# One encoder layer on one core: w_glu and p_ssm by seven block products, GpSimd's weight sums ahead of its gates

## The chip, the cores and the metric

The kernel runs on one core of a Trainium2 chip. The time is the device time of that core for one execution, in microseconds; the median of three runs is given. The engines are TensorE (PE, with PEld for its weight loads), VectorE (DVE), ScalarE (ACT), GpSimd (POOL) and SyncE (SP, which issues the loads).

## What is computed

One layer of a hybrid encoder over 512 prompt tokens and 64 sample tokens, 1024 channels. The part that the change touches:

```python
y_ssm = jax.nn.gelu(y_ssm + lp['ssm_d'].astype(jnp.float32) * u32)
y_ssm = (y_ssm * jax.nn.sigmoid(y_ssm @ lp['w_glu'])).astype(x.dtype)
mixed = jax.nn.sigmoid(g_s) * (y_ssm @ lp['p_ssm']) + jax.nn.sigmoid(g_a) * (att @ lp['p_att'])
x = x + rmsnorm(mixed @ lp['w_out'], lp['norm_mix_post'])
...
x = x + rmsnorm(jnp.square(jax.nn.relu(h @ lp['w_ff1'])) @ lp['w_ff2'], lp['norm_ff_post'])
```

w_glu and p_ssm are 1024 x 1024. Everything is float32.

## The kernel before

Products are made in fp32r: each operand is split into a high part (H, cut by ScalarE) and a low remainder (L, by VectorE), and a product is three matmuls, H x H, H x L and L x H. A weight is worked through in slabs of 128 output channels (128 x 1024 numbers, 512 KB). SyncE loads a raw slab into a slot `wraw`; ScalarE cuts it (`split_h`, L963), VectorE makes the remainder (`split_l`, L1663), and TensorE waits for `wl_done`. Four slabs of halves `wH`, `wL` rotate. Tokens are split into two halves of 288 (`HT`). `gemm` (L2401) makes one slab: 8 blocks of the depth x 3 x 2 halves = 48 matmuls.

The stages around the change, one after the other on TensorE: p_att, then w_glu (`T_GLU`, 8 slabs), then p_ssm (`T_PSSM`, 8 slabs), then w_out. In w_glu, ScalarE takes the sigmoid of slab j (L1310), VectorE multiplies it with y, which lies in `z` (L1982), and both cut the result y2 into `aH`, `aL` (L1013, L1677), the input of p_ssm. `z` is stored by time within a chunk, so its reads step through it (`by_time`). In p_ssm, VectorE multiplies the slab with the sigmoid of a gate that SyncE brings back from memory (L1989), adds the attention branch `m1` (L1992), and both cut the mixed result into `uH`, `uL`, the input of w_out. During the first w_out slab ScalarE squares the memory rows `memr` (L1323), which TensorE then transposes. GpSimd has no work in these stages.

In three of the four quarters of the feed-forward part a pair of w_ff1 slabs is made by seven block products instead of eight (`pair_products`, L3140): the pair is a 2 x 2 block matrix (two slabs x two halves of the depth), the tokens are two halves, and sums of blocks are multiplied. A product is 12 matmuls. GpSimd forms four sums of raw weight blocks into `comb` (T3, T2, T1, T4, L911 to L919), and ScalarE and VectorE cut six operands a pair: RA (a whole slab), T2, T1, T3, RB1 and T4 (half slabs). VectorE joins the products into the outputs, ScalarE copies one of them (p_1) out of PSUM (L1591).

Every engine works through its own list in order; waits on semaphores tie them.

## Time and profile before

| | |
|---|---|
| time, median of 3 runs | 1140.31 us (1140.18 to 1142.34) |
| span of the profiled execution | 1137.1 us |
| PE busy | 1122.3 us |
| DVE busy | 728.0 us |
| ACT busy | 574.5 us |
| POOL busy | 253.2 us |

The profiled execution's own time is not listed apart from its span. The span runs from the first to the last instruction; the time has about 3 us more. An engine's busy time is a sum over the whole program, in which stages with different limits follow each other. A row of a timeline has the start, the length and the instruction with its tiles (out<-in); "[x <-y]" is the idle time before it and what ended it. Instructions of one engine overlap a little, so their starts can be closer than their lengths.

### The profile page before, as it was taken

Reading aid. Unit: us, or ns where it says so; the run is one execution under the profiler, and the core shown is the slowest. Engines: PE = TensorE matmul, PEld = TensorE weight load, DVE = VectorE, ACT = ScalarE, POOL = GpSimd, SP = SyncE. Lnnn points to the kernel's source line nnn. Section 1 sums busy time; section 2 is a strip of 40 time slices with the busy share of each in tenths; the row PEclk is TensorE's granted clock in tenths of the full one; section 3 lists DMA queues with packets and bytes.
Section 4 is the critical chain, followed back from the end, with each engine's and each line's share of the span. In section 5 each row is a group of like instructions: output and inputs, shape, how many; then the busy total and the mean of one; then the engine's idle time right before and its main releaser. Section 6 shows DMA issues by size and latency. Waiting matters only on the chain.

```text
span 1137.1 us, 20194 instructions
## 1 busy us (share of the span) xinstructions
PE 1122.3 (99%) x8160; PEld 1039.2 (91%) x8160; DVE 728.0 (64%) x1195; ACT 574.5 (51%) x1084; POOL 253.2 (22%) x211
## 2 busy tenths in 40 slices
PE   9999999999999999999999999999999999999997
PEld 8999999999779999998889988899889889989986
DVE  6465899997784645554774463574859438626845
ACT  6564666654797533344655342554237416614642
POOL 1066888871110000000000000000044025013203
PEclk9999999999999999999999999999999999999999
DMA  9453336455103543353556204214422323242152
GB/s 218 136 145 86 98 97 174 137 152 169 44 2 99 174 132 94 116 180 107 177 157 208 70 19 130 74 40 167 117 68 76 112 74 95 74 129 68 56 174 84
DMA packets 154141, 128.76 MB, mean 113 GB/s; under 512 B 15712, under 2 KB 127264, under 8 KB 153728
## 3 DMA queue, kind: packets, MB, share of 16 engines
q1 hardware_dynamic: 142560, 114.76, 34.4%
q10 hardware_dynamic: 11488, 12.70, 3.3%
q8 instruction: 65, 1.06, 0.4%
q14 instruction: 28, 0.23, 0.1%
HBM read 110.73 MB, written 16.84 MB: 112 GB/s over the span
## 4 chain that ended last, share of the span: by engine, by line
PE 82%; ACT 7%; DVE 4%; POOL 2%; issue 2%; ACTq 2%; DMA 1%; POOLq 0%; DVEq 0%
PE gp L2416 24%; PE gp L2822 13%; PE sp L2822 13%; PE gp L3140 6%; PE sp L3140 6%; PE gp L2899 4%; PE gp L2726 3%; PE gp L3093 2%; PE sp L3058 1%; ACT sc L1237 1%; PE sp L2726 1%; ACTq L1114 1%; PE sp L2929 1%; ACT raw L1050 1%; POOL raw L809 1%
## 5 line engine op out<-in xcount | busy, mean ns | idle before, releaser
L1663 DVE TENSOR_TENSOR wL<-wraw,wH 128x1024 fp32r<-128x1024 f32 x139 | 180.9, 1303 | 156.8 <-ACT wH L963 154.4
L963 ACT ACTIVATE wH<-wraw 128x1024 fp32r<-128x1024 f32 x139 | 146.4, 1054 | 202.6 <-PE sp L2822 46.0
L2416 PE MATMUL gp<-aH,wH 128*128 128x288 f32 (+2 forms) x800 | 173.5, 298 | 0.0
L2416 PE MATMUL gp<-aH,wL 128*128 128x288 f32 (+2 forms) x800 | 171.4, 296 | 0.0
L2416 PE MATMUL gp<-aL,wH 128*128 128x288 f32 (+2 forms) x800 | 171.2, 296 | 0.0
L911 POOL TENSOR_TENSOR comb<-wraw 128x512 f32<-128x512 f32 x12 | 16.3, 1355 | 645.2 <-DMA wraw<-in_w_ff 578.3
L2416 PEld LDWEIGHTS gp<-aH,wH 128*128 128x128 f32 x800 | 129.3, 189 | 1.9 <-issue 1.8
L2416 PEld LDWEIGHTS gp<-aL,wH 128*128 128x128 f32 x800 | 129.8, 189 | 0.0
L2416 PEld LDWEIGHTS gp<-aH,wL 128*128 128x128 f32 x800 | 129.8, 189 | 0.0
L2822 PE MATMUL gp<-wH,fH 128*128 128x512 f32 x208 | 81.2, 390 | 0.0
L2822 PE MATMUL gp<-wL,fH 128*128 128x512 f32 x208 | 80.9, 389 | 0.0
L2822 PE MATMUL sp<-wH,fH 128*128 128x512 f32 x192 | 74.7, 389 | 0.0
L2822 PE MATMUL sp<-wL,fH 128*128 128x512 f32 x192 | 74.7, 389 | 0.0
L2822 PE MATMUL sp<-wH,fL 128*128 128x512 f32 x184 | 71.6, 389 | 0.0
L2260 DVE TENSOR_TENSOR wL<-comb,wH 128x512 fp32r<-128x512 f32 x48 | 38.4, 822 | 44.5 <-ACT wH L1565 44.5
L1565 ACT ACTIVATE wH<-comb 128x512 fp32r<-128x512 f32 x48 | 29.0, 622 | 56.6 <-PE sp L2822 47.4
L2822 PE MATMUL gp<-wH,fL 128*128 128x512 f32 x136 | 52.9, 389 | 0.0
L2822 PEld LDWEIGHTS gp<-wL,fH 128*128 128x128 f32 x208 | 39.1, 188 | 7.8
L2822 PEld LDWEIGHTS gp<-wH,fH 128*128 128x128 f32 x208 | 39.1, 188 | 7.8
L820 POOL TENSOR_TENSOR prod<-fb,btab 128x256 f32<-128x256 f32 x32 | 40.3, 1279 | 17.4 <-PE sp L2522 10.3
L2822 PEld LDWEIGHTS sp<-wL,fH 128*128 128x128 f32 x192 | 36.0, 188 | 7.5
L2822 PEld LDWEIGHTS sp<-wH,fH 128*128 128x128 f32 x192 | 36.0, 188 | 7.5
(549 smaller groups left out, 2839.7 us busy)
## 6 DMA issues: line engine op xcount, KB each, us to landing
wraw<-in_w_ff SPq DMA_DIRECT2D x64, 512.0 KB, 4.3
wraw<-in_w_in SPq DMA_DIRECT2D x36, 512.0 KB, 4.2
gates_scratch<-sq ACTq DMA_DIRECT2D x16, 288.0 KB, 2.2
gate<-gates_scratch SPq DMA_DIRECT2D x16, 288.0 KB, 4.2
wraw<-in_p_att SPq DMA_DIRECT2D x8, 512.0 KB, 4.2
wraw<-in_w_glu SPq DMA_DIRECT2D x8, 512.0 KB, 4.0
wraw<-in_p_ssm SPq DMA_DIRECT2D x8, 512.0 KB, 3.8
wraw<-in_w_out SPq DMA_DIRECT2D x8, 512.0 KB, 3.9
```

What stands on the lines that cost most here:

```text
L820: last = g.tensor_tensor(prod[:, i, :, 0:SB, :], fa, ba, ALU.mult)
L911: g.tensor_tensor(block("T3"), rb[:, 4:8, :], rb[:, 0:4, :], ALU.subtract).then_inc(comb_ready, 1)
L963: s_.activation(halves_of(t, j)[0][:], wraw[w][:], ACT.Copy).then_inc(wh_done, 1)
L1565: s_.activation(wH[i][:, k0:k1, :], operand_source(p, name), ACT.Copy).then_inc(wh_done, 1)
L1663: v.tensor_tensor(low[:], wraw[w][:], high[:], ALU.subtract).then_inc(wl_done, 1)
L2260: v.tensor_tensor(wL[i][:, k0:k1, :], operand_source(p, name), wH[i][:, k0:k1, :], ALU.subtract).then_inc(wl_done, 1)
L2416: last = mm(gp[:, b + h, 0:n], w[:, k, :], y[:, k, c0:c0 + n], start=(k == 0 and w is wH[s] and y is xh), stop=(k == KT - 1 and w is wL[s]))
L2726: last = mm(dst, w[:, k, :], y[:, k, :], start=(k == 0 and w is wH[j % 4] and y is xh), stop=(k == KT - 1 and y is xl))
L2822: last = mm(dst, y, wk, start=(k == 0 and m == 0), stop=(k == KT - 1 and m == len(passes) - 1))
L2899: last = mm(KV_BANK[n][m], y[:, k, c], w[:].rearrange("p k c -> p (k c)")[:, 512 * kk:512 * kk + 512], start=(k == 0 and w is wH[i] and y ...
L3093: last = mm(d[:, h, 0:HT], w[:, k, :], y[:, k, h * HT:(h + 1) * HT], start=(k == 0 and w is wH[s] and y is bH), stop=(k == KT - 1 and w is ...
L3140: last = mm(bank[name], w[:, k0 + k, :], y[:, kk + k, c], start=(name not in ("RA1", "RB1", "T4") and k == 0 and w is wH[i] and y is yH), ...
```

## The change

Of the four pairs of slabs of w_glu and of p_ssm, the first is still made slab by slab (`gemm`), and the other three by seven block products each, as in the feed-forward part. The pairs are numbered in one row: n = 0 to 2 in w_glu, 3 to 5 in p_ssm, 6 to 17 in the feed-forward part; in the loops below p = n + 1 and p = n - 2.

The products now add up in PSUM: RA0, then T2, T3 and T4 go into one bank on top of each other, T1 and RB1 into another. Between them ScalarE copies what has been reached (`keep`: p1 after RA0, p16 after T2, p5 after T1), and TensorE waits for p1 before T2, for p16 before T3, for p5 before RB1, and for VectorE's join "22" before T4. VectorE has three joins (11, 22, 12), ScalarE writes the fourth block itself (`out_21`). The feed-forward pairs use this order as well.

Sums of token blocks (S1 to S4) are formed from `z`: S1 and S3 by GpSimd, S2 and S4 by VectorE, and cut by ScalarE and VectorE. T1 is now summed in place in the raw slab. GpSimd also takes over the multiplication with the gate, in w_glu into `z` itself (`gate_ssm`), in p_ssm in `gate_out`. In each turn of its loop two weight sums (T3, T2) stand ahead of the two gates and two (T1, T4) behind. The cuts of y2 read `z`. Two more raw slots (`wraw5`, `wraw6`) take every other pair of slabs; a slot is loaded again when its pair's RB1 is cut and T4 summed (`wait_raw`). The gates of p_ssm are sigmoided in place. The memory rows are loaded near the end of p_ssm. Some semaphores are merged, and `in_order` makes the cut of an odd or even slab from 2 on wait for both gates of its pair.

```diff
-            for j in range(8):
-                free = (evac_dve, 8 + j - 1) if j < 2 else (evac_act, ACT_BEFORE[T_GLU] + j - 1)
-                gemm(T_GLU + j, j, bH, bL, free, IN_Y if j == 0 else None)
-            for j in range(8):
-                free = (evac_act, ACT_BEFORE[T_PSSM] + j - 1) if j < 2 else (evac_dve, 8 + j - 1)
-                gemm(T_PSSM + j, j, aH, aL, free, IN_Y2 if j == 0 else None)
+        def in_order(j):
+            return j + (2 if j >= 2 and j % 2 == 0 else 1)
...
+            def pair_products(n):
+                s, p, bank = stage(n), number(n), pair_bank(n)
+                xH, xL = ((bH, bL), (aH, aL), (bH, bL))[s]
+                lower, upper = slice(0, HT), slice(HT, TT)
+                turned = (xH, xL, 0, upper)
+                if s < 2:
+                    sums = {"T2": (zsH["S2"], zsL["S2"], 0, lower), "T1": (zsH["S1"], zsL["S1"], 0, lower),
+                            "T3": turned, "RB1": (zsH["S4"], zsL["S4"], 0, lower)}
+                else:
+                    sums = {"T2": (sumH[0], sumL[0], 0, lower), "T1": turned, "T3": (sumH[1], sumL[1], 0, lower),
+                            "RB1": (sumH[2], sumL[2], 0, lower)}
+                left = {"RA0": (xH, xL, 0, lower), "RA1": (xH, xL, 4, lower), "T4": (xH, xL, 4, upper), **sums}
+                dst = dict(zip(PRODUCTS, (bank[i] for i in (0, 1, 0, 2, 0, 2, 0))))
+                for name in PRODUCTS:
+                    operand = {"RA0": "RA", "RA1": "RA"}.get(name, name)
+                    pe.wait_ge(wl_done, operand_at(n, operand))
+                    if s < 2 and p == 1 and name in ("T2", "T1", "T3", "RB1"):
+                        pe.wait_ge(suml_done, 4 * s + {"T2": 1, "T1": 2, "RB1": 3, "T3": 4}[name])
+                    if name == "T2":
+                        pe.wait_ge(*kept_at(n, "p1"))
+                    if name == "T3":
+                        pe.wait_ge(*kept_at(n, "p16"))
+                    if name == "RB1":
+                        pe.wait_ge(*kept_at(n, "p5"))
+                    if name == "T4":
+                        pe.wait_ge(*join_at(n, "22"))
+                    i, k0, _ = operand_place(n, operand)
+                    k0 += 4 * (name == "RA1")
+                    yH, yL, kk, c = left[name]
+                    for k in range(4):
+                        for w, y in ((wH[i], yH), (wH[i], yL), (wL[i], yH)):
+                            last = mm(dst[name], w[:, k0 + k, :], y[:, kk + k, c],
+                                      start=(name in ("RA0", "RA1", "T1") and k == 0 and w is wH[i] and y is yH),
+                                      stop=(k == 3 and w is wL[i]), skip_group_check=True)
+                    last.then_inc(gemm_done, 1)
+            for j in range(2):
+                gemm(T_GLU + j, j, bH, bL, ((evac_dve, 8 + j - 1),), IN_Y if j == 0 else None)
+            pe.wait_ge(evac_dve, 8)
+            pair_products(0)
+            pe.wait_ge(evac_act, ACT_BEFORE[T_GLU] + 2)
+            pair_products(1)
+            pair_free(0)
+            pair_products(2)
+            for j in range(2):
+                gemm(T_PSSM + j, j, aH, aL, (join_at(1, "12"), (out21_done, 2)), IN_Y2 if j == 0 else None)
+            pair_free(2)
+            pair_products(3)
+            pe.wait_ge(evac_dve, DVE_BEFORE[T_WOUT])
+            pair_products(4)
+            pair_free(3)
+            pair_products(5)
...
@@ ScalarE, w_glu and p_ssm @@
-            for j in range(8):
-                split_h(T_GLU + j + AHEAD, j + AHEAD)
-                act.wait_ge(gemm_done, T_GLU + j + 1)
-                s_.activation(halves(raw[:, j % 2]), result(j), ACT.Sigmoid).then_inc(evac_act, 1)
-                cut_h(aH[:, j, :], sq[:, j % 2])
...
+            def keep(n, name):
+                product, dst, bank, use = {"p1": ("RA0", p_1, 0, "11"), "p16": ("T2", p_16, 0, "12"), "p5": ("T1", p_5, 2, "22")}[name]
+                act.wait_ge(gemm_done, product_at(n, product))
+                if n:
+                    act.wait_ge(*join_at(n - 1, use))
+                s_.activation(dst[:], pair_bank(n)[bank], ACT.Copy).then_inc(kept, 1)
+            def out_21(n, kind):
+                act.wait_ge(gemm_done, product_at(n, "T4"))
+                if n < 3:
+                    act.wait_ge(gated, 2 * number(n))
+                elif n < 6:
+                    act.wait_ge(mixed_ready, 2 * number(n))
+                s_.activation(raw[:, 0, HT:TT], pair_bank(n)[0], kind).then_inc(out21_done, 1)
+            def pair_sigmoid(n, e):
+                if e:
+                    act.wait_ge(*join_at(n, "22"))
+                    act.wait_ge(*join_at(n, "12"))
+                    s_.activation(raw[:, 1], raw[:, 1], ACT.Sigmoid).then_inc(evac_act, 1)
+                else:
+                    act.wait_ge(*join_at(n, "11"))
+            def y2_h(j):
+                act.wait_ge(gated, in_order(j))
+                s_.activation(aH[:, j, :].rearrange("p (c s) -> p c s", s=SB), by_time(z[:, j, :]), ACT.Copy).then_inc(in_h, 1)
+            z_sum_h(0, "S1")
+            z_sum_h(0, "S2")
+            z_sum_h(0, "S4")
+            glu_sigmoid(0)
+            operand_h(0, "T2")
+            y2_h(0)
+            operand_h(0, "T1")
+            operand_h(0, "T3")
+            glu_sigmoid(1)
+            z_sum_h(0, "S3")
+            operand_h(0, "RB1")
+            operand_h(0, "T4")
+            y2_h(1)
+            for p in (1, 2, 3):
+                n = p - 1
+                keep(n, "p1")
+                if p > 1:
+                    y2_h(2 * p - 1)
+                if p < 3:
+                    operand_h(n + 1, "RA")
+                else:
+                    split_h(T_PSSM, 0)
+                keep(n, "p16")
+                if p > 1:
+                    y2_h(2 * p - 2)
+                if p < 3:
+                    operand_h(n + 1, "T2")
+                else:
+                    split_h(T_PSSM + 1, 1)
+                pair_sigmoid(n, 0)
+                keep(n, "p5")
+                if p < 3:
+                    operand_h(n + 1, "T1")
+                    operand_h(n + 1, "T3")
+                else:
+                    gate_sig(8)
+                    gate_sig(9)
+                pair_sigmoid(n, 1)
+                if p < 3:
+                    operand_h(n + 1, "RB1")
+                    operand_h(n + 1, "T4")
+                else:
+                    operand_h(n + 1, "RA")
+                    operand_h(n + 1, "T2")
+                out_21(n, ACT.Sigmoid)
+            y2_h(7)
+            y2_h(6)
...
@@ GpSimd @@
+            def combine(n, names=("T3", "T2", "T1", "T4")):
+                ra, rb = pair_raw(n)
+                def free(name):
+                    if n not in (0, 6):
+                        pool.wait_ge(wl_done, operand_at(n - 1, name))
+                def block(name):
+                    return operand_source(n, name)
+                if "T3" in names:
+                    for t in (TWINS[n], TWINS[n] + 1):
+                        pool.wait_ge(w_loaded[raw_slot(t)], 16 * raw_uses(t))
+                    free("T3")
+                    g.tensor_tensor(block("T3"), rb[:, 4:8, :], rb[:, 0:4, :], ALU.subtract).then_inc(comb_ready, 1)
+                if "T2" in names:
+                    free("T2")
+                    pool.wait_ge(comb_ready, comb_at(n, "T3"))
+                    g.tensor_tensor(block("T2"), block("T3"), ra[:, 0:4, :], ALU.add).then_inc(comb_ready, 1)
+                if "T1" in names:
+                    g.tensor_tensor(block("T1"), rb[:, 0:4, :], ra[:, 0:4, :], ALU.subtract).then_inc(comb_ready, 1)
+                if "T4" in names:
+                    free("T4")
+                    pool.wait_ge(comb_ready, comb_at(n, "T2"))
+                    g.tensor_tensor(block("T4"), ra[:, 4:8, :], block("T2"), ALU.subtract).then_inc(comb_ready, 1)
+            def z_sum_1(i):
+                g.tensor_tensor(timed(zsum["S1"]), z_block(0, 1), z_block(1, 1), ALU.add).then_inc(z13_ready, 1)
+            def z_sum_3(i):
+                g.tensor_tensor(timed((bS3, uS3)[i]), z_block(0, 0), z_block(0, 1), ALU.subtract).then_inc(z13_ready, 1)
+            def gate_ssm(j):
+                p, e = j // 2, j % 2
+                if p == 0:
+                    pool.wait_ge(evac_act, ACT_BEFORE[T_GLU] + j + 1)
+                    pool.wait_ge(sum_ready, 2)
+                else:
+                    pool.wait_ge(*((evac_act, ACT_BEFORE[T_GLU] + 2 + p) if e else (out21_done, p)))
+                y = by_time(z[:, j, :])
+                g.tensor_tensor(y, raw[:, e].rearrange("p (c s) -> p c s", s=SB), y, ALU.mult).then_inc(gated, 1)
+            def gate_out(p, e):
+                n = 2 + p
+                if e:
+                    pool.wait_ge(*join_at(n, "12"))
+                else:
+                    pool.wait_ge(*join_at(n, "11"))
+                    pool.wait_ge(out21_done, n + 1)
+                pool.wait_ge(gsig_ready, 8 + 2 * p + e + 1)
+                g.tensor_tensor(raw[:, e], raw[:, e], gate[:, e], ALU.mult).then_inc(gated, 1)
+            pool.wait_ge(in_h, IN_Y + 1)
+            pool.wait_ge(gemm_done, g_count(T_PATT + 1))
+            z_sum_1(0)
+            pool.wait_ge(gemm_done, g_count(T_GLU))
+            z_sum_3(0)
+            combine(0, ("T3", "T2"))
+            gate_ssm(0)
+            combine(0, ("T1", "T4"))
+            gate_ssm(1)
+            for p in (1, 2, 3):
+                combine(p, ("T3", "T2"))
+                if p > 1:
+                    gate_ssm(2 * p - 1)
+                    gate_ssm(2 * p - 2)
+                combine(p, ("T1", "T4"))
+            gate_ssm(7)
+            gate_ssm(6)
+            pool.wait_ge(gemm_done, g_count(T_PSSM))
+            pool.wait_ge(gated, 8)
+            z_sum_1(1)
+            z_sum_3(1)
+            for p in (1, 2, 3):
+                if p < 3:
+                    combine(3 + p, ("T3", "T2"))
+                if p > 1:
+                    gate_out(p - 1, 1)
+                    gate_out(p - 1, 0)
+                if p < 3:
+                    combine(3 + p, ("T1", "T4"))
+            gate_out(3, 1)
+            gate_out(3, 0)
@@ VectorE @@
+            z_sums_24(0)
+            z_sum_l(0, "S2")
+            z_sum_l(0, "S1")
+            operand_l(0, "T2")
+            y2_l(0)
+            z_sum_l(0, "S4")
+            operand_l(0, "T1")
+            operand_l(0, "T3")
+            z_sum_l(0, "S3")
+            operand_l(0, "RB1")
+            operand_l(0, "T4")
+            y2_l(1)
+            for p in (1, 2, 3):
+                n = p - 1
+                if p > 1:
+                    y2_l(2 * p - 1)
+                if p < 3:
+                    operand_l(n + 1, "RA")
+                else:
+                    split_l(T_PSSM, 0)
+                if p > 1:
+                    y2_l(2 * p - 2)
+                out_11(n)
+                if p < 3:
+                    operand_l(n + 1, "T2")
+                    operand_l(n + 1, "T1")
+                else:
+                    split_l(T_PSSM + 1, 1)
+                out_22(n)
+                if p < 3:
+                    operand_l(n + 1, "T3")
+                out_12(n)
+                if p < 3:
+                    operand_l(n + 1, "RB1")
+                    operand_l(n + 1, "T4")
+                else:
+                    operand_l(n + 1, "RA")
+                    operand_l(n + 1, "T2")
+            y2_l(7)
+            y2_l(6)
...
@@ SyncE @@
+            def wait_raw(t):
+                before = raw_before(t)
+                n = pair_of(before)
+                if n is None:
+                    sp.wait_ge(wl_done, w_count(before + 1))
+                else:
+                    sp.wait_ge(wl_done, operand_at(n, "RB1"))
+                    sp.wait_ge(comb_ready, comb_at(n, "T4"))
+            def load_w(t, s, src):
+                assert s == raw_slot(t)
+                if t == T_GLU + 3:
+                    sp.wait_ge(evac_dve, 8)
+                elif t >= 2 and t != T_GLU + 2:
+                    wait_raw(t)
+                sp.dma_start(wraw[s][:], src).then_inc(w_loaded[s], 16)
```

In the lists below `p` is one of the copies p_1, p_16, p_5, `aH<-z` a cut of y2, `wH<-zcomb` a cut of a weight sum. ScalarE before, w_glu from the third slab on:

```order
L1310 ACTIVATE raw<-gp 128x576
L1013 ACTIVATE aH<-sq 128x576
L1292 ACTIVATE gsig<-gate 128x576
L963 ACTIVATE wH<-wraw 128x1024
L1310 ACTIVATE raw<-gp 128x576
L1013 ACTIVATE aH<-sq 128x576
L963 ACTIVATE wH<-wraw 128x1024
L1310 ACTIVATE raw<-gp 128x576
```

ScalarE now, w_glu pair n = 2. The three `p<-sp` are the copies p1, p16 and p5:

```order
L1426 ACTIVATE p<-sp 128x288
L1469 ACTIVATE aH<-z 128x576
L1087 ACTIVATE wH<-wraw 128x1024
L1426 ACTIVATE p<-sp 128x288
L1469 ACTIVATE aH<-z 128x576
L1087 ACTIVATE wH<-wraw 128x1024
L1489 ACTIVATE raw<-raw 128x288
L1426 ACTIVATE p<-sp 128x288
L1407 ACTIVATE gate<-gate 128x576 x2
L1486 ACTIVATE raw<-raw 128x576
```

Between two slab cuts there was a sigmoid and a cut of y2; now two cuts of y2 stand between and ahead of the copies that TensorE waits for, and the third copy stands behind the sigmoid of half a block.

GpSimd now, the turns p = 1 and p = 2 of w_glu and the start of the third (it had no instruction here):

```order
L978 TENSOR_TENSOR zcomb<-wraw 128x512
L982 TENSOR_TENSOR zcomb<-zcomb,wraw 128x512
L984 TENSOR_TENSOR wraw<-wraw 128x512
L988 TENSOR_TENSOR zcomb<-wraw,zcomb 128x512
L978 TENSOR_TENSOR zcomb<-wraw 128x512
L982 TENSOR_TENSOR zcomb<-zcomb,wraw 128x512
L1007 TENSOR_TENSOR z<-raw,z 128x144x4 x2
L984 TENSOR_TENSOR wraw<-wraw 128x512
L988 TENSOR_TENSOR zcomb<-wraw,zcomb 128x512
L978 TENSOR_TENSOR zcomb<-wraw 128x512
```

`zcomb<-` rows and `wraw<-wraw` are weight sums, `z<-raw,z` are gates: two sums, two gates, two sums in every turn.

## Rows read from the trace of the kernel before

**Rows 1.** The page's table: busy us, share of the span, instructions.
```profile
PE 1122.3 (99%) x8160; PEld 1039.2 (91%) x8160; DVE 728.0 (64%) x1195; ACT 574.5 (51%) x1084; POOL 253.2 (22%) x211
```

**Rows 2.** w_glu, p_ssm: us, then busy us of PE, PEld, DVE, ACT, POOL, then clock.
```profile
395.00:446.00 51.00, 51.00 (x385) 51.00 (x384) 23.98 (x24) 18.20 (x25) 0.00 (x0) 1.00 0.35 106
446.00:497.00 51.00, 51.00 (x385) 51.00 (x384) 28.15 (x38) 17.16 (x23) 0.00 (x0) 1.00 0.35 107
```

**Rows 3.** Chain of waits: start us, us, what; both stages, then one product.
```profile
394.76 102.40 PE gp L2416 x768
...
849.76 1.60 PE gp L3140 x12
```

**Rows 4.** Groups by form, ScalarE: busy us and mean ns; then its timeline, feed-forward.
```profile
L1565 ACT ACTIVATE wH<-comb 128x512 fp32r<-128x512 f32 x48 | 29.0, 622 | 56.6 <-PE sp L2822 47.4 <-PE sp L3140 6.6 <-PE gp L3140 2.6
...
L1304 ACT ACTIVATE bH<-z 128x576 fp32r<-128x576 f32 x8 | 9.8, 1228 | 0.0
...
L1013 ACT ACTIVATE aH<-sq 128x576 fp32r<-128x576 f32 x8 | 5.5, 686 | 10.2 <-DVE sq L1982 10.2
...
849.80 0.41 ACT L1584 ACTIVATE raw<-sp 128x288 f32<-128x288 f32 x1 [0.89 <-PE sp L3140]
850.11 1.05 ACT L1565 ACTIVATE wH<-wraw 128x1024 fp32r<-128x1024 f32 x1
```

**Rows 5.** Timeline of VectorE and of GpSimd, feed-forward: start us, us, instruction.
```profile
851.83 1.22 DVE L2260 TENSOR_TENSOR wL<-wraw,wH 128x1024 fp32r<-128x1024 f32 x1
852.96 0.68 DVE L2260 TENSOR_TENSOR wL<-comb,wH 128x512 fp32r<-128x512 f32 x1
853.56 0.45 DVE L2293 TENSOR_TENSOR raw<-sp,p 128x288 f32<-128x288 f32 x1
853.93 1.73 DVE L2260 TENSOR_TENSOR wL<-wraw,wH 128x512 fp32r<-128x512 f32 x1
855.58 1.79 DVE L2260 TENSOR_TENSOR wL<-comb,wH 128x512 fp32r<-128x512 f32 x1
...
858.52 1.81 DVE L2267 TENSOR_TENSOR fL<-sq,fH 128x512 fp32r<-128x512 f32 x1
...
853.81 1.29 POOL L911 TENSOR_TENSOR comb<-wraw 128x512 f32<-128x512 f32 x1 [6.01 <-DVE wL L2260]
855.25 1.56 POOL L914 TENSOR_TENSOR comb<-comb,wraw 128x512 f32<-128x512 f32 x1
856.78 1.73 POOL L916 TENSOR_TENSOR comb<-wraw 128x512 f32<-128x512 f32 x1
858.48 1.30 POOL L919 TENSOR_TENSOR comb<-wraw,comb 128x512 f32<-128x512 f32 x1
```

**Rows 6.** Groups by form, VectorE: cutting z, and cutting a plain buffer.
```profile
L1677 DVE TENSOR_TENSOR bL<-z,bH 128x576 fp32r<-128x576 f32 x8 | 9.5, 1185 | 2.7 <-ACT bH L1304 2.7
...
L1677 DVE TENSOR_TENSOR aL<-sq,aH 128x576 fp32r<-128x576 f32 x8 | 6.1, 759 | 6.0 <-ACT aH L1013 6.0
```

**Rows 7.** Timeline of GpSimd, early in the program.
```profile
60.31 1.42 POOL L809 TENSOR_TENSOR raw<-raw 128x576 f32<-128x576 f32 x1
...
72.40 1.55 POOL L820 TENSOR_TENSOR prod<-fb,btab 128x256 f32<-128x256 f32 x2
74.03 0.74 POOL L823 TENSOR_TENSOR xd<-prod 128x256 f32<-128x256 f32 x1
```

**Rows 8.** The page's DMA issues: KB each, us to landing.
```profile
wraw<-in_w_glu SPq DMA_DIRECT2D x8, 512.0 KB, 4.0
wraw<-in_p_ssm SPq DMA_DIRECT2D x8, 512.0 KB, 3.8
```

**Rows 9.** Timeline of ScalarE, first w_out slab: squaring the memory rows.
```profile
499.44 1.05 ACT L1323 ACTIVATE memn<-memr 128x1024 f32<-128x1024 f32 x1
```

**Rows 10.** Stretches at the end, with the columns of rows 2.
```profile
1129.00:1131.00 2.00, 1.93 (x9) 1.27 (x7) 1.19 (x2) 0.57 (x3) 0.89 (x1) 1.00 0.54 217
...
1135.00:1137.00 2.00, 0.00 (x0) 0.00 (x0) 0.00 (x0) 0.00 (x0) 0.00 (x0) 0.61 0.64 239
```

801 lines of the change are left out of this document (448 added, 353 removed).

## The prediction

> **What bounds the kernel now.** I read the page's table of engines first, then the stretches, then the chain. TensorE is busy for 1122.3 of 1137.1 us, and no other engine is above two thirds [rows 1]. In the two stages that the change rewrites it is busy the whole of both stretches: 51.00 of 51.00 us for w_glu and the same for p_ssm, while VectorE has 24 and 28 us, ScalarE 18 and 17, GpSimd nothing [rows 2]. The chain of waits shows the two stages as one unbroken piece, 768 matmuls of 288 columns in 102.40 us, 0.1333 us each [rows 3]. So a removed matmul is worth 0.1333 us at once, and a stall of TensorE costs its full length: nothing else stands ahead of it here. Every other engine is covered by half a stage of slack, and that slack is what the change spends.
>
> Durations come from one execution with a span of 1137.1 us. The runs have a median of 1140.3, so 3.2 us lie around the span, and I carry those over.
>
> **What is removed.** A pair of slabs takes 96 matmuls now, and 7 products x 12 = 84 after. Six pairs save 72 x 0.1333 = **9.6 us**. The same scheme already runs in the feed-forward quarters: a product of twelve lasts 1.60 us there as well [rows 3], so the price per matmul stays.
>
> **What is added, and where it lies.** I laid the instructions out in the new order, each at the first moment that its engine and its waits allow. Lengths: ScalarE 0.41 us for 288 columns (0.31 from start to start where the next follows at once; I take 0.1 off each length for that), 0.62 for 512, 1.05 for 1024, 0.69 for 576 [rows 4]. VectorE 0.69 (0.60) for 512, 1.22 (1.14) for 1024, 0.45 (0.37) from PSUM [rows 5]. The slabs of z are stored in another order than the token order, and reading them is dearer: 1.23 us against 0.69 on ScalarE, 1.19 against 0.76 on VectorE [rows 4, 6]. The cuts of y2 now read z, and so they pay this. GpSimd takes 1.29 us for a weight sum [rows 5] and 1.42 for 576 elements of two operands [rows 7]. A token sum has 1152 elements: twice 1.42, so 2.9 on GpSimd; on VectorE, reading z, twice 1.15, so 2.3.
>
> **GpSimd and VectorE take turns.** The decisive rows are in the feed-forward part. While GpSimd works through four weight sums (853.81 to 859.78), VectorE's cuts of 512 elements last 1.73, 1.79 and 1.81 us instead of 0.69, and each ends about 0.56 us after a GpSimd sum ends. VectorE's instructions that read PSUM stay at 0.45 [rows 5]. So a VectorE instruction with two operands in SBUF and a GpSimd one exclude each other: a turn of both takes 1.71 us, 1.29 and 0.42. I count VectorE's lengths 0.16 us shorter inside such turns.
>
> This is the load that the change adds. Per w_glu pair in the middle: GpSimd 4 x 1.29 + 2 gates x 1.42 = 8.0; VectorE's weight cuts 1.14 + 5 x 0.60 and y2 cuts 2 x 1.10 = 6.3. Together **14.3 us on one resource against 11.2 us of TensorE**. Before, all of it was VectorE's alone, with no GpSimd beside it. Let s be the time since the first w_glu matmul.
>
> *w_glu, pair 1* (TensorE could begin its T2 at s = 16.0). T2 adds into the bank of RA0, so it waits for ScalarE's copy of that bank (p1). ScalarE reaches the copy only after the cut of y2 slab 1, and this waits for GpSimd's gate product of slab 1. Ahead of it stand, in turns, GpSimd 2.9 + 4 x 1.29 + 2 x 1.42 = 10.9 and VectorE's two token sums, two cuts of token sums, a weight cut and a y2 cut, 2 x 2.14 + 2 x 1.10 + 0.44 + 0.94 = 7.9 (each less 0.16; a cut of 1152 elements is taken at 1.26): s = 18.8. Cut 1.14, copy 0.31, handing over 0.15: T2 at 20.4, a wait of **4.4**. Then RB1 waits for the copy of T1's bank (p5). ScalarE has it behind a sigmoid of the first output block, and that block is joined by VectorE behind 7.2 us of its own cuts and four GpSimd sums at 1.29 - 0.16 = 1.13 net: 18.8 + 11.7 = 30.5, plus join, sigmoid, copy 1.2: 31.7 against 25.2, **6.5**.
>
> *Pair 2.* The second copy (p16) is behind the cuts of y2 slabs 3 and 2, which wait for both gates, which GpSimd makes after two weight sums: **1.5**. Then VectorE's order (y2 cut 1.10, a turn 1.13, weight cut 1.14, y2 cut 1.10, join 0.37) plus sigmoid and copy make RB1 wait **2.8**.
>
> *Pair 3.* Here the order in the change's name decides: the weight sums stand ahead of the gates, and their raw slabs are late. Slots 5 and 6 are free only once the half RB1 of this pair is cut, which ScalarE does behind the sigmoid that needs pair 2's RB1 product. From the end of that product: join 0.5, sigmoid 0.6, cuts 0.5, 0.6 and handing over 0.7 = 2.9; second load issued 0.45 later, landing after 4.1 (page: w_glu 4.0, p_ssm 3.8 [rows 8]); two sums 2.65, two gates 2.85, y2 cut 1.14, slab cut 0.96, copy 0.4: 15.4. TensorE wants T3 after 8.0, so **7.5**, and again **2.8** at RB1. No turn-taking is needed for this one.
>
> *p_ssm, slab 1.* It needs all of y2 by its seventh step. The two last gates, then VectorE's two y2 cuts in turns with GpSimd's two token sums of 2.9: **7.0**. *Pair 1*: VectorE must form two sums (2 x 2.3), cut four (4 x 1.26) and mix two slabs first: **4.8**, and 1.3 at T4. *Pair 2*: p16 behind mixed slab 3, which waits for GpSimd's gates behind two sums: **4.9**, and 1.0. *Pair 3*: 0.8 + 0.3 + 0.5. *w_out*: the memory rows were squared during the first w_out slab [rows 9]; now this starts after the last mixed cut and the first transposes wait **3.2**.
>
> The feed-forward pairs get another order too: the p1 copy is needed one product after RA0's end, not two. ScalarE, after T4: output 0.3, relu, square and cut at 0.70 each, copy 0.3, so 2.8 against 3.2. It is covered by 0.4 us; without that cover it would cost what is missing, nine times over. I take nothing.
>
> Sum: w_glu 25.5, p_ssm 20.6, w_out 3.2 = 49.3 us of waits, less 9.6: **+39.7**, so 1140.3 + 39.7 = **1180 us**.
>
> One price no row has is GpSimd reading z. Its product that reads one operand at a stride (L820) takes 0.78 us for 256 elements against 0.74 for its neighbour without [rows 7]: hardly anything. I take the low end.
> The Trainium skill's page "GPSIMD Engine Reference" (section "Performance pitfalls for Q7 kernels") puts reads at strides over 8 bytes at half as much again. By it, gates cost 2.1 and token sums 4.3 us, and an estimate of the sum is 1195; the row speaks against it.
>
> **Rivals.**
> *The clock falls as well.* TensorE has been at the upper level (granted clock 1.00, 2.4 GHz) in every stretch shown. But after its last matmul at 1130.9 the clock stood at 0.61 on average over 1135 to 1137, so it had begun to fall within 6 us of idling [rows 10]. Six of my waits last 4.4 to 7.5 us. At the lower level twelve matmuls take 3.2 instead of 1.6 us; if four waits each bring two such products, that adds 12.8: **1193**.
> The page "TensorE: Matmul & The Clock Gate" of the Trainium skill (section "Part 1: The HAM clock gate") says that an idle TensorE is put to half rate and gets full rate back only once it has been busy again. By it this rival is right for the longest waits.
> *The turns cost nothing here*, because VectorE and GpSimd fall out of step. Then only chains of waits stay: 1.1, 1.6, 7.5, 1.8 in w_glu, 1.6, 3.2, 1.7, 1.0, 1.6 in p_ssm, 3.2 in w_out: 24.3, less 9.6: **1155**. Against it: in the rows the turns hold through all four sums.
> *All is hidden.* VectorE and ScalarE had 27 and 33 us to spare in w_glu; if every copy came in time, 1140.3 - 9.6 = **1130.7**. This is the other side. It decides when the waits stay under 9.6 us together; pair 3's chain alone, all of it loads and instructions with rows, takes 7.5 of that.
> *Slow GpSimd reads*, the estimate above: about **1195**.
>
> **How the numbers follow.** Forecast 0.44 (1168 to 1189), clock 0.18, slow reads 0.08, turns free 0.15, all hidden 0.11, something beyond 1200 in 0.04. The range 1150 to 1198 leaves out the hidden case and the last, and small ends of the others. Below -0.2% (about what a measurement of this kernel can tell from no change): 0.10, nearly all of the hidden case; within: 0.03; above: 0.87.
>
> **What the profile after would show.** TensorE's idle time of about 50 us, nearly all between the first w_glu and the first w_out matmul; longest before T2 of pair 1, RB1 of pair 1, T3 of w_glu pair 3 and in p_ssm slab 1, released by ScalarE's copies p or by VectorE's cuts. Products of 1.60 us in between, or 3.2 if the clock falls. VectorE's cuts at 1.7 us and more beside GpSimd in w_glu. GpSimd's sum for p_ssm pair 1 waiting for its raw slab. The feed-forward quarters as long as before, 45 us. I am wrong if w_glu lasts under 51 us, or if the copies stand ahead of their products by more than a product.

## The result, and the profile after

The changed kernel takes 1190.35 us (median of 4 runs, 1189.68 to 1192.66), the kernel before 1140.24 us. The ratio is 1.044, with a 95% interval of 1.042 to 1.045: 50.1 us slower. The forecast was 1180 with a band of 1168 to 1189, its range 1150 to 1198.

The page's table, the answer to [rows 1]: TensorE has 72 matmuls less and is yet 5.5 us longer busy, and the span is 50.8 us longer.

```profile
PE 1127.8 (95%) x8088; PEld 1042.2 (88%) x8088; DVE 787.0 (66%) x1211; ACT 611.9 (52%) x1164; POOL 342.8 (29%) x253
```

The stretches of w_glu, p_ssm and the start of w_out (columns of [rows 2]: us, then busy us and instructions of PE, PEld, DVE, ACT, POOL, then the granted clock) answer to [rows 2]. TensorE was busy 51.00 of 51.00 us; now it is busy 38.45 of 51, then 30.05 of 50, and the granted clock is 0.86 and 0.74 where it was 1.00.

```profile
396.00:447.00 51.00, 38.45 (x251) 37.84 (x250) 45.25 (x31) 22.14 (x34) 36.99 (x17) 0.86 0.29 84
447.00:497.00 50.00, 30.05 (x181) 29.30 (x180) 29.87 (x21) 18.06 (x25) 22.36 (x10) 0.74 0.15 43
497.00:548.00 51.00, 42.63 (x288) 40.65 (x288) 40.21 (x51) 24.27 (x42) 23.03 (x14) 0.97 0.41 128
```

The timeline of TensorE, only the rows that begin after idle time (start, length, instruction, in brackets the idle time and what ended it), from w_glu to w_out. These thirteen rows are the result.

```profile
418.80 0.58 PE L3189 MATMUL sp<-zsHS,wH 128*128 128x288 f32 x1 [6.15 <-ACT p L1426]
...
429.73 0.58 PE L3189 MATMUL sp<-zsHS,wH 128*128 128x288 f32 x1 [4.45 <-ACT p L1426]
...
445.72 0.38 PE L3189 MATMUL gp<-zsHS,wH 128*128 128x288 f32 x1 [1.95 <-ACT p L1426]
...
465.64 0.58 PE L3189 MATMUL sp<-bH,wH 128*128 128x288 f32 x1 [8.62 <-ACT p L1426]
...
469.92 0.58 PE L3189 MATMUL sp<-zsHS,wH 128*128 128x288 f32 x1 [1.06 <-ACT p L1426]
...
489.80 0.85 PE L2770 MATMUL gp<-aH,wH 128*128 128x288 f32 x2 [10.28 <-DVE aL L1915]
...
504.39 0.37 PE L3189 MATMUL sp<-zsHS,wH 128*128 128x288 f32 x1 [1.43 <-ACT p L1426]
...
512.93 0.37 PE L3189 MATMUL sp<-aH,wH 128*128 128x288 f32 x1 [1.93 <-DVE raw L2229]
...
525.66 0.37 PE L3189 MATMUL gp<-aH,wH 128*128 128x288 f32 x1 [3.01 <-ACT p L1426]
...
529.81 0.38 PE L3189 MATMUL gp<-aH,wH 128*128 128x288 f32 x1 [0.71 <-DVE raw L2229]
...
539.05 0.37 PE L3189 MATMUL sp<-aH,wH 128*128 128x288 f32 x1 [1.05 <-ACT p L1426]
...
542.94 0.38 PE L3189 MATMUL sp<-aH,wH 128*128 128x288 f32 x1 [0.24 <-DVE raw L2229]
...
553.89 1.06 PE L3216 MATMUL sp<-ident,memn 128*128 128x128 f32 x8 [2.74 <-DVE memn L2384]
```

The tile tells which product it is: `zsHS` with the bank's first matmul is T2 or RB1, `bH` is T3, `gp<-aH` at 489.80 is the first p_ssm slab. In order: T2 and RB1 of w_glu pair 1, RB1 of pair 2, T3 and RB1 of pair 3, the p_ssm slab, T2 and T4 of p_ssm pair 1, T3 and T4 of pair 2 and of pair 3, and the memory rows. From the first w_glu matmul (396.53) to the first w_out matmul (544.62) it takes 148.09 us, before 102.40. I call this the stage time below. It holds 696 matmuls, 92.8 us at 0.1333 each, and waits of 40.9 us. The 14.4 us that are left are what the matmuls took longer at the lower clock: the product behind the wait of 8.62 takes 3.23 us, and a product without a wait at full clock 1.60.

The whole sum against the span: stage time +45.7; the start of w_out +4.5 (2.7 of waiting for the memory rows, the other 1.8 at a clock of 0.83); a wait of 1.47 us in p_att; the feed-forward part -1.2; 0.3 in other places. Together +50.8.

### The profile page after: what moved, and what is told of

Its sections match the earlier page's. It is cut to its first block, busy times and chain, and to the rows that moved or that the text cites. A ratio compares the mean times of both kernels' runs of the same rounds, so it can differ in the third digit from the quotient of the medians.

```text
span 1187.9 us, 20347 instructions
## 1 busy us (share of the span) xinstructions
PE 1127.8 (95%) x8088; PEld 1042.2 (88%) x8088; DVE 787.0 (66%) x1211; ACT 611.9 (52%) x1164; POOL 342.8 (29%) x253
## 3 DMA queue, kind: packets, MB, share of 16 engines
q8 instruction: 64, 1.05, 0.4%
## 4 chain that ended last, share of the span: by engine, by line
PE 71%; DVE 10%; ACT 9%; POOL 4%; issue 4%; ACTq 2%; DMA 1%; DVEq 0%; SPq 0%; POOLq 0%
PE gp L2770 14%; PE gp L3228 13%; PE sp L3228 12%; PE sp L3189 7%; PE gp L3189 6%; PE gp L3306 4%; PE gp L3080 3%; DVE wL L2207 2%; PE gp L3502 2%; PE sp L3465 1%; ACT sc L1352 1%; ACTq L1229 1%; DVE aL L1915 1%; PE sp L3336 1%; DVE zsLS L2254 1%
## 5 line engine op out<-in xcount | busy, mean ns | idle before, releaser
L1087 ACT ACTIVATE wH<-wraw 128x1024 fp32r<-128x1024 f32 x127 | 133.7, 1055 | 195.8 <-PE sp L3228 57.1
L2770 PE MATMUL gp<-aH,wH 128*128 128x288 f32 (+1 forms) x704 | 153.7, 300 | 10.3 <-DVE aL L1915 10.3
L2770 PE MATMUL gp<-aL,wH 128*128 128x288 f32 (+1 forms) x704 | 151.3, 297 | 0.0
L2770 PE MATMUL gp<-aH,wL 128*128 128x288 f32 (+1 forms) x704 | 151.2, 297 | 0.0
L2770 PEld LDWEIGHTS gp<-aH,wH 128*128 128x128 f32 x704 | 114.5, 190 | 12.4 <-DVE aL L1915 10.5
L2770 PEld LDWEIGHTS gp<-aL,wH 128*128 128x128 f32 x704 | 115.0, 190 | 0.0
L2770 PEld LDWEIGHTS gp<-aH,wL 128*128 128x128 f32 x704 | 114.9, 190 | 0.0
L2207 DVE TENSOR_TENSOR wL<-wraw,wH 128x512 fp32r<-128x512 f32 (+1 forms) x54 | 60.6, 1123 | 44.0 <-ACT wH L1418 43.9
L1418 ACT ACTIVATE wH<-wraw 128x512 fp32r<-128x512 f32 (+1 forms) x54 | 41.5, 768 | 62.4 <-PE sp L3228 43.3
L3189 PE MATMUL sp<-bH,wH 128*128 128x288 f32 x128 | 39.1, 306 | 8.6 <-ACT p L1426 8.6
```

Source lines behind the costliest of these rows:

```text
L1087: s_.activation(halves_of(t, j)[0][:], wraw[w][:], ACT.Copy).then_inc(wh_done, 1)
L1418: s_.activation(wH[i][:, k0:k1, :], operand_source(n, name), ACT.Copy).then_inc(wh_done, 1)
L2207: v.tensor_tensor(wL[i][:, k0:k1, :], operand_source(n, name), wH[i][:, k0:k1, :], ALU.subtract).then_inc(wl_done, 1)
L2770: last = mm(gp[:, b + h, 0:n], w[:, k, :], y[:, k, c0:c0 + n], start=(k == 0 and w is high and y is xh), stop=(k == KT - 1 and w is low))
L3189: last = mm(dst[name], w[:, k0 + k, :], y[:, kk + k, c], start=(name in ("RA0", "RA1", "T1") and k == 0 and w is wH[i] and y is yH), stop= ...
```

## Experiments

Each kernel is the changed one with one edit, unless it says otherwise. The median of the kernel before, run beside them, was 1140.5 to 1140.7.

**1. Gates ahead of the weight sums.** The order that gives the change its name, turned round on GpSimd, in both stages:

```diff
             for p in (1, 2, 3):
-                combine(p, ("T3", "T2"))
                 if p > 1:
                     gate_ssm(2 * p - 1)
                     gate_ssm(2 * p - 2)
+                combine(p, ("T3", "T2"))
```

> GpSimd makes the two gate products of a turn ahead of the weight sums T3 and T2, in w_glu and in p_ssm; nothing else is changed. Theory (the wait of 8.62 us before T3 of the third w_glu pair is the chain raw slot, load, two weight sums, two gates, cut of y2, copy p16): the gates no longer stand behind the late load, so this wait goes, and with it the two products at the lower clock that follow it; behind it RB1 of the same pair waits up to 2.8 us. The wait in the first p_ssm slab stays at 10 us. Time 1176 to 1181, 9 to 14 us below the changed kernel's 1190.35. Rival (what costs is the sum of GpSimd's and VectorE's work, whatever its order): the wait before T3 only moves to the next places, and the time stays within 3 us of 1190.

1181.03 us (2 runs), 9.3 less, at the edge of what I expected. The stage time is 136.54, 11.6 less; the difference to 9.3 is that in this execution the first w_glu matmul came at 398.56 instead of 396.53, a part of the program that the edit does not touch. TensorE's rows after idle time around the third pair:

```profile
447.77 0.38 PE L3189 MATMUL gp<-zsHS,wH 128*128 128x288 f32 x1 [3.10 <-ACT p L1426]
...
461.09 0.37 PE L3189 MATMUL sp<-zsHS,wH 128*128 128x288 f32 x1 [1.66 <-ACT p L1426]
...
480.98 0.85 PE L2770 MATMUL gp<-aH,wH 128*128 128x288 f32 x2 [11.67 <-DVE aL L1915]
```

The row at T3 (`sp<-bH`, 8.62) is gone, RB1 waits 1.66, and the p_ssm slab 11.67. The theory stands: that wait was the load, two weight sums, two gates. The chain of the changed kernel shows it link by link (start, us, what):

```profile
445.72 3.03 PE gp L3189 x12
...
451.81 5.15 DMA wraw<-in_p_ssm
...
457.08 1.27 POOL zcomb L978
...
458.49 1.26 POOL zcomb L982
...
461.35 1.70 POOL z L1007
...
464.15 1.05 ACT wH L1087
465.20 0.30 ACT p L1426
...
465.64 3.23 PE sp L3189 x12
```

The slot is loaded from 451.81 to 456.96, the sums take until 459.75, and only then come the gates, whose inputs ScalarE had written by 450.1 and 451.4. The chain begins with the RB1 product of pair 2 (first row). It ran at a granted clock of 0.54, 2.82 us from its first matmul to the next product's; that matters in experiment 4.

**2. Token sums of p_ssm behind the last cuts of y2.**

```diff
-            pool.wait_ge(gated, 8)
+            pool.wait_ge(in_l, IN_Y2 + 8)
             z_sum_1(1)
             z_sum_3(1)
```

> GpSimd's two token sums of p_ssm (S1, S3) wait until VectorE has made the last two cuts of y2. Theory (the wait of 10.28 us in the first p_ssm slab is VectorE's two cuts, each held up by one of GpSimd's token sums of 4.4 and 5.4 us): the wait in the slab falls to about 3 us, the two cuts last about 1.1 us each instead of 9.5 together; but the sums are needed for T2 of the first p_ssm pair, whose wait of 1.43 us grows to 10 or more. Time about as before, 1188 to 1194. Rival (VectorE's cuts are slow for another reason, as the reading of z at strides): cuts stay at 4 us and more, and the wait in the slab stays at 8 us or more.

1191.66 us (2 runs), stage time 148.74. VectorE's two last cuts of y2, first in the changed kernel with GpSimd beside them, then here:

```profile
480.23 9.52 DVE L1915 TENSOR_TENSOR aL<-z,aH 128x576 fp32r<-128x576 f32 x2 [0.72 <-ACT aH L1469]
```

```profile
479.11 4.36 POOL L992 TENSOR_TENSOR zsumS<-z 128x1152 f32<-128x1152 f32 x1
483.42 5.41 POOL L996 TENSOR_TENSOR uS<-z 128x1152 f32<-128x1152 f32 x1
```

```profile
479.78 2.19 DVE L1915 TENSOR_TENSOR aL<-z,aH 128x576 fp32r<-128x576 f32 x2 [0.72 <-ACT aH L1469]
```

```profile
482.12 4.31 POOL L992 TENSOR_TENSOR zsumS<-z 128x1152 f32<-128x1152 f32 x1 [3.60 <-DVE aL L1915]
```

Two cuts last 9.52 us beside the two sums and 2.19 without them: each cut ended 0.8 to 0.9 us after a sum did (the sums end at 483.47 and 488.83). So reading z at strides is not what makes them slow. GpSimd waits as well: with VectorE out of the way S1 takes 4.31 us (last row) and S3 4.78, so of the 5.41 above some 0.6 are a wait for VectorE's first cut. The wait in the slab fell from 10.28 to 2.96, and T2 of the next pair, which needs the sums, waits 10.78 instead of 1.43. The wait was moved and nothing was won, as expected (T3 of p_ssm pair 2 also waits longer, 4.56 instead of 3.01).

**3. The clock held up, with too much.** TensorE is kept busy ahead of the long waits by matmuls of the identity into a bank that nobody reads:

```diff
                 for name in PRODUCTS:
                     operand = {"RA0": "RA", "RA1": "RA"}.get(name, name)
+                    fill(FILL.get((n, name), 0))
```

> Ahead of the six longest waits TensorE makes matmuls of the identity with itself into a PSUM bank that nobody reads: 40 before T2 and 28 before RB1 of w_glu pair 1, 12 before T3 of pair 2, 60 before T3 of pair 3, 75 ahead of the seventh step of the first p_ssm slab, 20 before T3 of p_ssm pair 2. They take about 0.13 us each and end before the wait would. Theory (14.4 us of the change's cost are matmuls at the lower clock after the waits): the granted clock is 1.00 or near it through both stages, the products behind the waits take 1.60 us instead of 3.2, and the time is 8 to 14 us below 1190.35, so 1176 to 1182; some of it comes back as longer waits, where the chain did not run over TensorE. Rival (the chain runs through the other engines, and the slow products are hidden in it): the clock is 1.00, but the waits grow by as much, and the time stays within 3 us of 1190.

1194.01 us (2 runs), stage time 149.79. A fill matmul took 0.23 us, not 0.13, so the fills outlasted the waits: 235 of them are 54 us, where 34.5 were to be filled. I had also taken the wait of 1.95 us for T3 of pair 2; it is that pair's RB1, so one fill stood where there was no wait. The clock did what was wanted, 1.00 from 396 to 535, but with some 19 us of spare matmuls too many the run decides nothing.

**4. The clock held up, with less.** The same edit with smaller numbers; the seven of pair 2 again stand before T3, where there is no wait.

> As the filled kernel before it, but the identity matmuls, which turned out to take 0.21 us each and so outlasted the waits, are fewer: 22 before T2 and 16 before RB1 of w_glu pair 1, 7 before T3 of pair 2, 36 before T3 of pair 3, 44 in the first p_ssm slab, 12 before T3 of p_ssm pair 2, so 4.7, 3.4, 1.5, 7.7, 9.4 and 2.6 us in waits of 6.15, 4.45, 1.95, 8.62, 10.28 and 3.01. Theory (14.4 us of the cost are matmuls at the lower clock, and they lie on the path): clock 1.00 through both stages, what is left of the waits plus the fill is about what the waits were, and the time is 1176 to 1180. Rival (the path runs through the other engines, slow products are hidden): waits grow by what the products gain, time 1187 to 1191.

1191.72 us (3 runs, 1187.70 to 1191.73), stage time 149.00 against 148.09 in the profiled one of 1191.73. The granted clock was 1.00, 0.94, 1.00 and 1.00 in the four stretches up to 500, in the changed kernel 0.92, 0.80, 0.76 and 0.74:

```profile
396.00:418.80 22.80, 22.80 (x179) 22.80 (x178) 20.17 (x9) 8.42 (x11) 19.41 (x7) 1.00 0.32 96
418.80:447.00 28.20, 23.51 (x171) 22.95 (x169) 23.16 (x21) 12.19 (x20) 16.91 (x11) 0.94 0.27 75
447.00:480.00 33.00, 27.47 (x214) 27.14 (x215) 13.92 (x16) 12.88 (x23) 12.68 (x8) 1.00 0.23 65
480.00:500.00 20.00, 19.28 (x160) 19.09 (x159) 19.09 (x10) 7.26 (x8) 9.98 (x2) 1.00 0.02 3
```

The product at T3 of pair 3 now takes 1.85 us, not 3.23. Yet TensorE is released at nearly the same moments as without the fills (rows after idle time, filled kernel):

```profile
420.54 0.37 PE L3199 MATMUL sp<-zsHS,wH 128*128 128x288 f32 x1 [1.28 <-ACT p L1426]
...
431.48 0.37 PE L3199 MATMUL sp<-zsHS,wH 128*128 128x288 f32 x1 [2.35 <-ACT p L1426]
...
467.94 0.37 PE L3199 MATMUL sp<-bH,wH 128*128 128x288 f32 x1 [2.46 <-ACT p L1426]
...
472.22 0.37 PE L3199 MATMUL sp<-zsHS,wH 128*128 128x288 f32 x1 [2.45 <-ACT p L1426]
```

Counted from the first w_glu matmul (398.22 here, 396.53 there): T2 of pair 1 at 22.3 in both, RB1 at 33.3 and 33.2, T3 of pair 3 at 69.7 and 69.1, its RB1 at 74.0 and 73.4. The p_ssm releases differ by 0.9 us at most. The theory fell, and the rival holds in the main: in these stages the path runs through ScalarE, VectorE, GpSimd and the loads, and what TensorE loses to the lower clock it would otherwise have waited. Waits and slow matmuls are together 55.3 us, and nearly all of it is delay by the other engines.

One slow product is an exception. The RB1 product of w_glu pair 2 stands at the head of the chain of experiment 1. It takes 1.66 us here instead of 2.82, and the load for p_ssm starts 1.1 us earlier behind it. That T3 of pair 3 is not released earlier is chance, because this load took 6.67 us instead of 5.15:

```profile
452.57 6.67 DMA wraw<-in_p_ssm
```

In the kernel of experiment 2, which has no fills, the same product happened to run at full clock too, its load took 5.25 us, and T3 came at 68.2 after the first w_glu matmul instead of 69.1. So of the 14.4 us about 1 lies on the path, not 8 to 14. Why this load was slower is not known. In w_out, where the transposes wait 2.74 us and TensorE is busy without a break behind them, the slow matmuls are taken to cost their full 1.8 us; no run tested that.

**5. The gates of w_glu on VectorE.**

```diff
-            gate_ssm(0)
             combine(0, ("T1", "T4"))
-            gate_ssm(1)
...
-                    gate_ssm(2 * p - 1)
-                    gate_ssm(2 * p - 2)
...
+                    gate_ssm(2 * p - 1)
+                    gate_ssm(2 * p - 2)
                     y2_l(2 * p - 1)
```

The lines taken out are GpSimd's, those put in VectorE's; the gates of the first and the last pair move in the same way.

> The eight gate products of w_glu are made by VectorE, two at a time ahead of its cuts of y2, instead of by GpSimd; p_ssm as it was. Theory (GpSimd and VectorE exclude each other, so it matters little which of them works, while GpSimd's order no longer puts the gates behind the late weight sums): the wait before T3 of the third w_glu pair falls from 8.62 to under 1 us, RB1 of that pair waits up to 4, T2 of pair 1 up to 8, the first p_ssm slab waits 10 as before; the waits of the two stages together fall by 3 to 8 us. Time 1180 to 1188. Rival (GpSimd is the bound by its own slowness and VectorE has room): T2 and RB1 of pair 1 also lose most of their waits, and the time falls below 1176.

1183.44 us (2 runs), stage time 140.23, 7.9 less. T3 of pair 3 does not wait, its RB1 waits 2.13, T2 of pair 1 7.93, the p_ssm slab 10.64. As expected: a load taken from GpSimd and given to VectorE helps where GpSimd's order held the gates back, and at T2 of pair 1 it costs 1.8. In pair 2, T3 now waits 3.25 us where it did not wait before, and RB1 0.7 less.

**6. All token sums on VectorE.**

```diff
             def z_sums_24(i):
+                dve.wait_ge(gemm_done, g_count((T_GLU, T_PSSM)[i]))
+                v.tensor_tensor(timed(zsum["S1"]), z_block(0, 1), z_block(1, 1), ALU.add).then_inc(z13_ready, 1)
                 dve.wait_ge(z13_ready, 2 * i + 1)
-                dve.wait_ge(gemm_done, g_count((T_GLU, T_PSSM)[i]))
```

S3 likewise, behind S4.

> GpSimd's token sums S1 and S3 are made by VectorE, in a row with its own two, in both stages; GpSimd begins with the weight sums. Theory (both engines exclude each other; VectorE needs 2.2 us for such a sum and GpSimd 4.4): T2 of w_glu pair 1 waits about as before, 6 to 8 us; in the first p_ssm slab VectorE's two cuts last 1.1 us each and the wait falls from 10.28 to about 3, of which T2 of p_ssm pair 1 takes back 4 to 8; time 1184 to 1190. Rival (no exclusion, GpSimd is merely slow): without GpSimd's 4.8 us sum everything behind it is earlier, T2 of w_glu pair 1 waits under 3 us, and the time falls below 1180.

1186.14 us (3 runs, 1183.22 to 1186.92), 4.2 less. The profiled one is the slowest of the three and only 2.8 us shorter than the changed kernel's; there the stage time has 1.9 less and p_att 1.5. VectorE makes a token sum (S1) in 2.26 us, the changed kernel's GpSimd needed 4.77 for S3, and 4.31 for S1 (experiment 2):

```profile
396.84 2.26 DVE L2223 TENSOR_TENSOR zsumS<-z 128x1152 f32<-128x1152 f32 x1
399.13 2.24 DVE L2225 TENSOR_TENSOR zsumS<-zsumS,z 128x1152 f32<-128x1152 f32 x1
```

```profile
396.77 4.77 POOL L996 TENSOR_TENSOR bS<-z 128x1152 f32<-128x1152 f32 x1 [28.95 <-PE gp L3080]
```

T2 of pair 1 waits 6.78, the slab 3.08, T2 of p_ssm pair 1 7.48. Each is inside what the exclusion asks for. Beside it the wait in p_att is gone: it was this pair of rows of the changed kernel, VectorE's cut of a weight slab that normally lasts 1.2 us, held up by GpSimd's first token sum.

```profile
363.49 5.42 DVE L1901 TENSOR_TENSOR wL<-wraw,wH 128x1024 fp32r<-128x1024 f32 x1
```

```profile
362.42 5.40 POOL L992 TENSOR_TENSOR zsumS<-z 128x1152 f32<-128x1152 f32 x1 [17.05 <-ACT bH L1463]
```

**7. Both, gates first and token sums on VectorE.** The edits of 1 and 6 together.

> Both earlier edits together: GpSimd's gates ahead of its weight sums in both stages, and all four token sums on VectorE. Theory (the two act at different places: T3 of the third w_glu pair, and the first p_ssm slab): the gains of 9.3 and 4.2 us add up, time 1175 to 1179. Rival (they act on the same wait): 1180 or more.

1177.56 us (3 runs), stage time 134.97: 13.1 less, where the two alone gave 11.6 and 1.9. They add up within 0.4 us; the kernel is still 37 us above the kernel before.

**8. w_glu alone by seven products.** p_ssm as before, the feed-forward order kept.

```diff
-        TWINS = [t0 + 2 * p for t0 in (T_GLU, T_PSSM) for p in (1, 2, 3)] + \
+        TWINS = [t0 + 2 * p for t0 in (T_GLU,) for p in (1, 2, 3)] + \
...
-            for j in range(2):
-                gemm(T_PSSM + j, j, aH, aL, (join_at(1, "12"), (out21_done, 2)), IN_Y2 if j == 0 else None)
-            pair_free(2)
-            pair_products(3)
+            for j in range(8):
+                gemm(T_PSSM + j, j, aH, aL, (join_at(1, "12"), (out21_done, 2)) if j < 2 else ((evac_dve, 8 + j - 1),), IN_Y2 if j == 0 else None)
```

> w_glu by seven products as in the changed kernel, p_ssm slab by slab as before (VectorE multiplies with the gate, GpSimd idle there), new order of the feed-forward pairs kept. Theory (each stage pays for its own chains, and the wait of 8.6 us before T3 of the third w_glu pair exists only because weight sums for p_ssm stand ahead of the gates): T2 of pair 1 waits 6.2 and RB1 4.5, T3 of pair 2 about 2 and its RB1 2 to 3, T3 of pair 3 not at all, its RB1 2, the first p_ssm slab about 3 instead of 10.3, and none later. Together 20 to 22 us less 4.8 saved, with 1.5 in p_att and -1.2 in the feed-forward part: time 1155 to 1159. Rival (the third pair's wait and the slab's are w_glu's own): 1168 or more.

1158.50 us (3 runs, 1157.66 to 1162.55), stage time 121.29. The waits are 6.14 and 4.45 in pair 1, 1.95 at RB1 of pair 2 (its T3, for which I had expected 2, does not wait), 1.54 at RB1 of pair 3, and the slab's:

```profile
471.05 0.53 PE L2697 MATMUL gp<-aH,wH 128*128 128x288 f32 x2 [2.95 <-DVE aL L1876]
```

So w_glu by seven products costs 19 us against the kernel of the next experiment, and p_ssm another 32: 26.8 in the stage time and the 4.5 at w_out. Among them is the 8.62 that stood in w_glu, where the gates had waited for p_ssm's weights. Saved matmuls are worth 4.8 in each.

**9. The feed-forward order alone.** w_glu and p_ssm slab by slab, all else of the change kept.

```diff
-        TWINS = [t0 + 2 * p for t0 in (T_GLU, T_PSSM) for p in (1, 2, 3)] + \
-                [T_FF + 16 * q + 2 * p for q in range(1, QUARTERS) for p in range(4)]
+        TWINS = [T_FF + 16 * q + 2 * p for q in range(1, QUARTERS) for p in range(4)]
```

> The changed kernel with w_glu and p_ssm made slab by slab again, GpSimd idle there, memory rows loaded and squared as before; the new order of the feed-forward pairs, which adds up in PSUM, is kept. Theory (all of the cost lies in w_glu and p_ssm, and the new order gains: 44.63 to 44.76 us a quarter against 45.03 to 45.17): 1138.7 to 1139.5, 1.2 us below the kernel before, a ratio of 0.999. Rival (something else of the change, merged waits or the loads, costs too): 1141 or more.

1139.18 us (11 runs) against 1140.47 (15 runs), ratio 0.999 with an interval of 0.9981 to 0.9999. Stage time 102.40. So this version beats both kernels, the kernel before by 0.1%. The interval ends close to 1, but the traces show the same 1.2 us: a quarter takes 44.63 us here and 45.03 before. The chain over a feed-forward quarter is four pairs of 84 matmuls without a break, where before about 0.2 us was lost twice a quarter at a product's start (these took 1.79 us instead of 1.60):

```profile
846.05 11.15 PE sp L2888 x84
857.20 11.16 PE gp L2888 x84
868.36 11.16 PE sp L2888 x84
879.52 11.16 PE gp L2888 x84
```

```profile
872.08 1.60 PE gp L3140 x12
873.68 1.79 PE sp L3140 x12
```

**10. GpSimd busy beside an unchanged w_glu.** To the kernel of experiment 9 comes spare work on GpSimd, from the first w_glu matmul on: 32 additions of two operands, or 64 copies.

```diff
+            for i in range(32):
+                g.tensor_tensor(zcomb[:, 0, :], zcomb[:, 1, :], zcomb[:, 2, :], ALU.add).then_inc(spare, 1)
+                pool.wait_ge(spare, i + 2)
```

> The kernel with the feed-forward part alone (1139.18 us), and from the start of w_glu GpSimd makes 32 sums of two 512-element operands, from and into a spare buffer; nobody waits for them there. Theory (a VectorE instruction with two SBUF operands and a GpSimd one exclude each other): VectorE's slab cuts in w_glu last about 2.4 us instead of 1.2, each ending after a GpSimd sum has ended, its multiplications and cuts of y2 likewise; with three such instructions a slab VectorE needs 6.8 us for a slab of 6.4, and TensorE waits 1 to 5 us in all: time 1140 to 1144. ScalarE's lengths stay. Rival (no exclusion): VectorE's lengths stay, GpSimd's are 1.29 us, time 1139.

> As the one before it, but GpSimd makes 64 copies of 512 elements, one operand each. Theory (it is GpSimd's second operand that needs what VectorE's two operands need): VectorE's slab cuts keep their 1.2 us, time 1139 to 1139.5. Rival (every GpSimd instruction excludes VectorE's): VectorE's cuts last 1.7 us or more beside the copies.

1139.50 us (9 runs) and 1138.97 us (9 runs), neither told apart from the kernel without (1139.18). The stretch of w_glu, the additions, the copies, then the kernel without either:

```profile
395.00:446.00 51.00, 51.00 (x384) 51.00 (x383) 33.95 (x24) 18.34 (x24) 47.63 (x26) 1.00 0.37 114
```

```profile
395.00:446.00 51.00, 51.00 (x384) 51.00 (x384) 29.11 (x24) 18.23 (x24) 47.18 (x50) 1.00 0.37 109
```

```profile
395.00:446.00 51.00, 51.00 (x383) 51.00 (x382) 23.10 (x24) 18.35 (x24) 0.00 (x0) 1.00 0.40 120
```

VectorE's 24 instructions take 33.95 us instead of 23.10 beside additions, and 29.11 beside copies; ScalarE keeps its 18.3. The lengthening is there, but by 0.45 us an instruction on average, not the 1.2 I had expected for the slab cuts (they last 1.97 instead of 1.23), and TensorE waited for none of it: my 1 to 5 us were wrong. VectorE had more than 20 us of slack here and still has 17. Part of the price falls on the other side: GpSimd's additions last 1.87 us, not 1.29. With spare work one behind the other VectorE begins somewhere within an addition and waits out only what is left of it, and the next addition waits for VectorE. The copies lengthen too (0.25 each), so that they spare VectorE wholly is refuted. They wait for VectorE as the additions do: two of them take 1.29 us where VectorE is idle and 2.56 beside its cuts. That a copy costs VectorE less only because it is half as long is likely, but not shown.

## Why the prediction was right, and where it was not

Direction, places and causes came out as forecast, and the time lies in the range. It lies 10 us above the forecast and just outside its band of 1168 to 1189, nearer to two rivals (1193 and 1195). That the clock rival's number is so near is luck, because what it adds is mostly hidden.

**The saving.** Saved: 9.6 us forecast, and 72 matmuls are gone; a product at full clock still lasts 1.60 us [rows 3]. Right.

**The waits.** w_glu: 25.5 forecast (4.4, 6.5, 1.5 and 2.8, 7.5 and 2.8), 22.2 measured (6.15, 4.45, 0 and 1.95, 8.62 and 1.06). p_ssm: 20.6 forecast (7.0; 4.8 and 1.3; 4.9 and 1.0; 0.8, 0.3 and 0.5), 18.7 measured (10.28; 1.43 and 1.93; 3.01 and 0.71; 1.05, 0 and 0.24). w_out: 3.2 forecast, 2.74 measured. Places and releasers are those that were named, except that the second copy (p16) of w_glu pair 2 was in time, and experiments 1, 2, 6 and 8 took away or moved the larger waits one at a time. But the waits are only what was left after TensorE ran slowly. Counted as I had forecast it, by how much later than a TensorE at full clock would ask for it each product is released, the delay is 55.3 us in the two stages, against 46.1 in my sum. Outside them w_out has 1.3 us more than forecast, and p_att 1.5 that I had not counted.

**The step that was mis-sized** is "One price no row has is GpSimd reading z ... I take the low end". I counted 2.9 us for a token sum; left alone they take 4.31 (S1) and 4.78 (S3), and in the changed kernel 4.77, 4.36 and 5.41. At T2 of pair 1 that is 1.9 (forecast at 20.4 after the first w_glu matmul, released at 22.3), in the first p_ssm slab 4.31 + 4.78 - 5.8 = 3.3. Together 5.2 of the missing 9.2. The slab is released 11.9 us late against my 7.0; most of the other 1.6 are the last two gates, which took 4.40 us beside two of VectorE's weight cuts instead of my 2.85.

The next term is the wait for T3 of w_glu pair 3: 10.3 us late instead of 7.5. The RB1 product at the head of its chain took 2.82 us, not 1.60, at the lower clock (1.2); the load took 5.15 us from its start, where I had 4.1 (1.0); the two gates took 3.33, where I had 2.85 (0.5). T2 of p_ssm pair 1, on the other hand, was 3.4 late and not 4.8. The other places add 1.0, which makes the 9.2.

A gate product on z, with one operand at a stride, lasts 1.67 us, one on plain buffers 1.41; I had 1.42 for both. GpSimd's rows in the changed kernel, a pair of gates of w_glu and a pair of p_ssm (3.33 and 2.82 us for two):

```profile
459.71 3.33 POOL L1007 TENSOR_TENSOR z<-raw,z 128x576 f32<-128x576 f32 x2
...
544.53 2.82 POOL L1018 TENSOR_TENSOR raw<-raw,gate 128x576 f32<-128x576 f32 x2 [10.17 <-DVE raw L2235]
```

The row I leaned on (L820, [rows 7]) has one operand at a stride and said nothing about two.

The rule of the Trainium skill's page "GPSIMD Engine Reference" (section "Performance pitfalls for Q7 kernels"), half as much again for reads at strides over 8 bytes, was the better price for the token sums: 4.31 and 4.78 against twice 1.41 are 1.53 and 1.70 times. For a gate, with one strided operand of two, it was 1.18 times. The estimate that I made by it, 1195, missed by 5 us on the far side, my own by 10.

**The clock rival** was half right. The clock fell as it said, to 0.50 over the product behind the wait of 8.62. That slow products add 12.8 us was wrong: where the other engines set the pace they cost about 1 us (experiment 4), and 1.8 in w_out. I added a cost of TensorE to a sum in which TensorE was no longer the bound.

**Taking turns** [rows 5] held where the kernel's own work met: 9.52 us for two cuts (experiment 2), 5.42 for a cut of 1.2 in p_att. This last place I had missed altogether: the first token sum is released in p_att, by ScalarE's first cut of z (bH), and stands beside VectorE's cut of a weight slab; TensorE waited 1.47 us.

**The feed-forward part.** "I take nothing" was wrong to the other side: the new order gains 1.2 us (experiment 9). The trace of before has the rows with stalls of 0.2 us at a product's start (experiment 9); I had not read them.

**All is hidden** fell where its turning point said: the third pair's wait for T3 alone is 8.62 us, nearly all of the 9.6. **The turns cost nothing** fell with experiments 2 and 6.

## What to carry to other kernels

Seven products instead of eight save an eighth of the matmuls of a pair and put a chain of copies, sums and joins between them. Before a load is shifted to an idle engine, ask what it shares with the one that is relieved, and put what others wait for ahead of what itself waits for a load. A slow TensorE costs next to nothing while the others set its pace (about 1 us of 14.4 here), so a clock term is not to be added whole to a sum in which they do; what counts are the slow products that the others' chain starts from.

## What the runs showed of the hardware that I had not expected

- A VectorE instruction with two SBUF operands waits out a GpSimd instruction of several us: 5.42 us for a slab cut that takes 1.22 alone, beside a token sum of 5.40. GpSimd waits for VectorE too: its first weight sum of w_glu took 3.05 us beside VectorE's token sums, and the one of the chain in experiment 1, beside none, 1.27.
- GpSimd needs 4.31 us (S1) or 4.78 (S3) for 1152 elements with both operands at a stride, VectorE 2.26 (S1); with plain operands GpSimd would need 2.82 by an estimate (twice 1.41).
- Holding TensorE's clock at 0.94 to 1.00 by spare matmuls changed the release of its products by 0.6 us at most in w_glu, and the stage time by +0.9.
- A matmul of the identity with itself, 128 columns of float32, took 0.23 us, where the kernel's own of 288 columns take 0.133.
